# The SSD score block behind a whole gate piece instead of between its halves

## The reference, cut to what matters

```
hn = rmsnorm(h, norm_mix_w)
q, k, v, z, xbc, dt_raw = split(hn @ w_in)           # z: 1024 columns, q: 512
xbc = silu(causal_conv(xbc));  x, B, C = split(xbc)
cb = einsum('bclgn,bcsgn->bcgls', C, B)              # scores of B and C
y_diag = einsum(cb, decay_in, X)                     # X = x * dt, near products
y_off  = einsum(C, prev_state, exp(a_cum))           # what earlier chunks give
y = (y_diag + y_off + d_skip * x) * silu(z)
y = y * rsqrt(mean(y*y)) * norm_w
```

## Time and profile before

| | |
|---|---|
| median of three runs | 776.09 us |
| profiled execution | 776.6 us, span 774.7 us |
| TensorE busy | 761.6 us (98%) |
| VectorE busy | 520.6 us (67%) |
| ScalarE busy | 409.8 us (53%) |
| GpSimd busy | 99.2 us (13%) |

### The profile page before, as it was taken

One profiled execution on the slowest core, in us unless ns is written; L12 is line 12 of the kernel. 1 busy time (PEld: TensorE's weight loads), 2 busy tenths in 40 slices (PEclk: granted clock), 3 DMA queues, 4 the chain that ended last, 5 costly groups with the idle time before them and its releaser, 6 DMA issues.

```text
span 774.7 us, 12888 instructions
## 1 busy us (share of the span) xinstructions
PE 761.6 (98%) x4980; PEld 669.7 (86%) x4980; DVE 520.6 (67%) x828; ACT 409.8 (53%) x616; POOL 99.2 (13%) x74
## 2 busy tenths in 40 slices
PE   9999999999999999999999999999999999999997
PEld 8998877799978887999786799899877999999996
DVE  6985556666665558577966976898757755555554
ACT  5544445453665453445676547874545544444443
POOL 2241000000100004111400209701000000000002
PEclk9999999999999999999999999999999999999999
DMA  9865653344664655576743375744327575656541
GB/s 333 320 215 183 210 170 108 111 152 126 200 232 156 188 163 163 184 209 192 253 144 109 113 231 195 260 131 144 130 61 230 187 240 183 211 174 209 174 153 55
DMA packets 77660, 139.54 MB, mean 180 GB/s; under 512 B 7185, under 2 KB 15649, under 8 KB 77601
## 3 DMA queue, kind: packets, MB, share of 16 engines
q1 hardware_dynamic: 75744, 132.15, 53.0%
q0 software_dynamic: 1856, 6.57, 2.6%
HBM read 134.90 MB, written 1.06 MB: 176 GB/s over the span
## 4 chain that ended last, share of the span: by engine, by line
PE 86%; DVE 6%; issue 3%; ACT 2%; POOL 2%; DMA 1%; POOLq 0%; ACTq 0%; SPq 0%; DVEq 0%
PE acc L1100 13%; PE acc L1102 12%; PE acc L1101 12%; PE acc L1108 12%; PE acc L1110 12%; PE acc L1109 12%; DVE w_lo L827 2%; PE acc L1413 1%; PE acc L1447 1%; PE acc L1281 1%; PE acc L1386 1%; PE acc L1326 1%; PE acc L1397 1%; POOL stats L2453 1%; DMA raw<-in_w_in_even 1%
## 5 line engine op out<-in xcount | busy, mean ns | idle before, releaser
L827 DVE TENSOR_TENSOR w_lo<-raw,w_hi 128x1024 fp32r<-128x1024 f32 (+1 forms) x224 | 275.9, 1249 | 166.5 <-ACT w_hi L807 90.6
L1108 PE MATMUL acc<-x_hi,w_hi 128*128 128x256 f32 x840 | 234.9, 280 | 0.9 <-DVE w_lo L827 0.5
L1110 PE MATMUL acc<-x_hi,w_lo 128*128 128x256 f32 x840 | 232.2, 276 | 0.0
L1109 PE MATMUL acc<-x_lo,w_hi 128*128 128x256 f32 x840 | 232.1, 276 | 0.0
L807 ACT ACTIVATE w_hi<-raw 128x1024 fp32r<-128x1024 f32 (+1 forms) x128 | 133.6, 1045 | 127.2 <-PE acc L1110 66.9
L797 ACT ACTIVATE w_hi<-raw 128x1024 fp32r<-128x1024 f32 x109 | 116.1, 1065 | 105.8 <-PE acc L1110 51.6
L1108 PEld LDWEIGHTS acc<-x_hi,w_hi 128*128 128x128 f32 x840 | 157.7, 188 | 3.5 <-issue 3.2
L1109 PEld LDWEIGHTS acc<-x_lo,w_hi 128*128 128x128 f32 x840 | 157.8, 188 | 0.8 <-issue 0.5
L1110 PEld LDWEIGHTS acc<-x_hi,w_lo 128*128 128x128 f32 x840 | 157.7, 188 | 0.0
L1100 PE MATMUL acc<-w_hi,cat_hi 128*128 128x512 f32 x272 | 108.9, 400 | 0.2 <-DVE w_lo L827 0.2
L1102 PE MATMUL acc<-w_hi,cat_lo 128*128 128x512 f32 x272 | 106.2, 391 | 0.0
(11 more groups left out here) (303 smaller groups left out, 900.2 us busy)
## 6 DMA issues: line engine op xcount, KB each, us to landing
raw<-in_w_ff SPq DMA_DIRECT2D x32, 1024.0 KB, 5.3
raw<-in_w_in_even SPq DMA_DIRECT2D x28, 1024.0 KB, 5.1
raw<-in_w_in_odd SPq DMA_DIRECT2D x16, 1024.0 KB, 5.5
raw<-in_w_in SPq DMA_DIRECT2D x16, 1024.0 KB, 5.8
raw<-in_w_out_even SPq DMA_DIRECT2D x12, 1024.0 KB, 5.2
raw<-in_w_out SPq DMA_DIRECT2D x4, 1024.0 KB, 5.3
raw<-in_w_in_even SPq DMA_DIRECT2D x4, 512.0 KB, 6.0
raw<-in_w_ukv_even SPq DMA_DIRECT2D x8, 256.0 KB, 3.2
```

The lines of the kernel that those rows point to most:

```text
L827: ins = eng.tensor_tensor(lo, r, hi.bitcast(F32), ALU.subtract)
L1108: pe.matmul(o, wh[k][:, fs], hi[:, ka, :], start=start and f % 2 == 0, stop=False, skip_group_check=True)
L1109: pe.matmul(o, wh[k][:, fs], lo[:, ka, :], start=False, stop=False, skip_group_check=True)
L1110: ins = pe.matmul(o, wl[k][:, fs], hi[:, ka, :], start=False, stop=stop, skip_group_check=True)
```

## The change

In the order of steps, the five steps that stood between the halves of z1a (`ssd_cb` 0, `ssd_rows` 0, `ssd_seg` 1, `ssd_xs` 1, `ssd_far` 0) stand behind its second half. The halves of the six other pieces are as they were.

```
@@ -476,9 +476,12 @@
     for f, sts in zip(parts[2:] + [second_v], between):
         one, two = by_halves(f)
         one()
+        if f is parts[2]:
+            two()
         for st in sts:
             step(*st)
-        two()
+        if f is not parts[2]:
+            two()
         if ("ssd_gate", 0) in sts:
             step("ssd_scale", 0)
```

## The result

The changed kernel takes 779.5 us (777.7 to 780.4, eight executions), the kernel before 776.6 (776.0 to 777.6, eight): ratio 1.0032, interval 1.0024 to 1.0041. The medians lie 2.9 us apart (by the interval 1.9 to 3.2) where +1.2 was forecast, and 779.5 lies outside my range of 776.0 to 778.4.

What follows compares the result with a forecast made beforehand. TensorE, busy 761.6 of 774.7 us, was taken as the bound, so only its waits counted: -0.68 at the block and +1.85 before y_far, taken as +1.2 on 776.09, gave 777.3 us, range 776.0 to 778.4.

Steps and rivals of the forecast that it cites:

- Steps 1 to 3: Block to y_far: wait before the block goes (-0.68 us), VectorE's queue keeps its length, TensorE stands 1.85 us before y_far.
- step 1: At the score block: it starts 2.04 us later, directly behind z1a without a wait, gaining 0.68 us.
- C: Rival at VectorE's held lower part before the mask: it waits for ScalarE's copy, +1.7 us, 777.8 us; chance 0.12.
- B: Rival at the L1269 wait: half the delay, 0.6 us, is absorbed later, giving 776.7 us; chance 0.10.
- Step 4: Sum for the stage: y_far starts 1.17 us late (-0.68 + 1.85), bounds +0.9 to +1.6, taken as +1.2.
- step 2: VectorE's queue: qa's first lower part is hidden, the second takes its place; x_far still 8.65 us behind the block's start.
- I take the cost as 0: TensorE's clock after the 1.85 us wait before y_far: judged to stay full, costing 0 us.
- D: Rival at the hole before y_far: clock drops to 1.2 GHz, costing 0.42 us, +1.6 in all, 777.7 us; chance 0.04.

Runs made afterwards that it cites:

- a_again: The changed kernel run again with no edit: 778.35 us, against 776.81 for the kernel before.
- b_hole3: The kernel before with x_far made four times over by VectorE, for a hole ahead of y_far: 781.99 us, against 776.9 before.
- b_turn2: The kernel before with two more VectorE products ahead of the scale of y, lengthening TensorE's wait at L1269: 781.1 us, ratio 1.0044 to 1.0069.
- a_far_late: The changed kernel with only the y_far step moved, behind z1b's second half: 776.81 us, against 776.66 before.
- a_low_late: The changed kernel with VectorE's held lower part (qa's second half) moved behind x_far: 776.95 us, against 776.66 before.
- a_both: The changed kernel with x_far made ahead of the block and qa's held lower part behind the turned rows of x: 776.58 us, against 776.81 before.
- b_hole1: The kernel before with x_far made twice over by VectorE: 778.36 us, against 776.9 before.
- a_best: The changed kernel with x_far ahead of the block and both of qa's lower parts held behind the turned rows of x: 777.06 us, against 776.91 before.

## Why the prediction was wrong

Steps 1 to 3, the sum of the waits, held. The block began 2.04 us later against the stage's start (500.27 - 493.94 against 497.67 - 493.38), as in step 1. Near products started 4.94 us behind the block (forecast 5.07), y_far 8.47 (8.65), the hole was 1.80 (1.85). The held part cost nothing ahead of the mask (C didn't happen), and nothing was absorbed later (B): the distance between the two traces stays what it was from the near products on. Step 4 said +1.17; y_far began +0.99 late, and a_again has a stage of +0.96. One detail of step 2 was off and hidden: qa's first lower part took 2.37 us, not 1.22, so VectorE stood idle for 0.30 us before the masks and not for some 1.6.

**The step that failed is the clock**: "I take the cost as 0". The runs put 1.3 to 1.7 us in its place (a_again against the first profile 1.55, b_hole3 1.68, b_turn2 1.3 by their stages; 1.8 between the medians of the two heaps), in 11 of 19 executions. In the first set the median is one of these: its 779.5 is before + 1.0 + 1.8. The prediction's own sign for D, matmuls behind the hole that take twice as long, came true: 2.79 us for y_far instead of 1.37. I had seen the mechanism (rival D) and gave it 4 in 100 and 0.42 us. Both came from misreading one row:

- The chance. In the last 4.7 us the clock was full for nearly four, and I took this for the time an idle TensorE always keeps it. It is one draw. The end of the span is the same work in all 14 traces, and counted from the last matmul's end the clock fell after 4.6 us in the kernel before, but after 2.2 in the changed kernel, whose last 4.7 us are

```profile
773.00:777.70 4.70, 0.00 (x0) 0.00 (x0) 1.25 (x4) 1.69 (x4) 0.57 (x2) 0.67 0.58 223
```

  and after 2.4 to 5.2 in the twelve others. In the stages, counted from the hole's start, the fall came after about 1.4 us in the changed kernel (506.9 to 508.3), 3.8 in b_hole3 (507.5 to 511.3), 2.7 in b_turn2 (536.2 to 539.0), and not at all in a_again.
- The price. The last 0.85 us at half clock end where the record ends, not where the clock would have come back. In the changed kernel it stood at half from 508.3 to 511.7, 3.4 us of which 0.4 were still hole; the other 3.0, on y_far and dense matmuls, cost half of that, 1.5.

With a chance of one half and 1.6 us the case would have stood beside my forecast, and the range would have reached 780. A median over two outcomes is that of whichever came more often in the set: of the other heap in the first eight executions, of the lower one in a_again. +1.2 was the lower heap.

The Trainium skill, "TensorE: Matmul & The Clock Gate", section "HAM oscillation — how this bites in real kernels", says that an idle gap puts TensorE back to half clock and the next matmuls start cold, but it says so of gaps longer than any hole here. The kind of loss agrees with b_hole3 and b_turn2; the length doesn't, since the clock fell in 11 of 19 executions with a hole of 1.8 us, and the runs decide. Its section "What's actually happening" also says that the chip's watch is not tied to the kernel's start, so that the same program varies from run to run. The two heaps of the changed kernel, and the 2.2 to 5.2 us at the span's end, would be such a variation; no run here shows that this is their cause.

## What to carry to other kernels

A wait that is moved is not only added up: if it becomes longer than any that TensorE has between its matmuls, ask for the clock, and price it with a stretch that has both edges in the record, or with a deliberate hole of that size, before saying zero. Where a fall is a matter of chance, read the list of executions with their clocks before the median. And when a step is put behind half a piece more of TensorE's work, the partner engine's queue to the next wait must be as long as what is left between them: here 8.65 us stood against 6.8 by the forecast, 8.47 against 6.67 in the trace, and moving the consumer too (a_far_late) removed the loss.

## What the runs showed of the hardware

- A hole of 1.5 to 1.8 us was enough to halve the clock in 14 of 24 executions, 0.86 or less in none of 33 (a_low_late, a_both, b_hole1), 2.8 in 5 of 5 and 3.2 in at least 4 of 5; and 2.0 us at another place in none of 8. Spare matmuls in the hole kept it in 11 of 11.
- From the last matmul of the span to the fall it took 2.2 to 5.2 us in 14 traces with the same work at their end. Once fallen it stood at half for about 3.4 us (the changed kernel, b_hole3, b_turn2).
- The clock can fall when TensorE is already working again, one us after the hole (b_hole3).
- VectorE's subtraction of two SBUF operands took 2.37 us instead of 1.22 when it was issued at 499.13 while GpSimd was in its own subtraction. In the changed kernel GpSimd's row is

```profile
495.59 4.83 POOL L830 TENSOR_TENSOR w_lo<-raw,w_hi 128x1024 fp32r<-128x1024 f32 x2 [1.53 <-ACT w_hi L800]
```

  which ends at 500.42, and VectorE ended 1.08 later. Products with a PSUM operand kept 1.22 beside GpSimd. The Trainium skill, "SBUF — State Buffer", section "SBUF: two separate sides", says that a VectorE operation with two SBUF inputs and a GpSimd operation exclude each other, and the one that comes second waits for the whole of the other; the trace agrees to within 0.15 us (1.08 against 1.22), and so does a_best, where x_far, with two SBUF operands too, took 2.17 us and ended 1.09 behind GpSimd. It also fits a_both, whose masks began 2.46 us behind the block's start and not 1.53: x_far stood behind that subtraction (2.35 us).
